# Bidirectional attention inside a two-layer encoder: the order of transposes, value matmuls and evictions within a slot

## The chip, the cores and the metric

The kernel runs on one core of one Trainium2 chip. The metric is the time of one execution on the device in microseconds. Three executions of the kernel before took 5469.95, 5459.16 and 5456.58 us, a median of 5459.16 us. Engines are named as the profile names them: PE is TensorE (PEld its weight loads), DVE VectorE, ACT ScalarE, POOL GpSimd, SP the engine that issues the DMAs.

## The reference, cut to what matters

Two layers run over a prompt of 512 tokens and a sample of 2048, each with three groups of heads: a recurrent one, an attention, and a gated one. The change touches the attention alone. It has six heads; queries and keys have 96 features, values 64, all in float32, and nothing is masked:

```python
def bidir_attention(q, k, v):
    ...
    def one_block(q_blk):
        s = jnp.einsum('bqhd,bkhd->bhqk', q_blk.astype(jnp.float32), kf) * scale
        p = jax.nn.softmax(s, axis=-1).astype(v.dtype)
        return jnp.einsum('bhqk,bkhd->bqhd', p, v)
```

Prompt and sample attend each to itself: 512 queries over 512 keys, and 2048 over 2048.

## The kernel before, in words

Each layer runs through stages with a barrier behind each: feature projection, token projection, recurrent scan, attention (`mla_attention`), output projection. In the attention stage four engines run programs of their own and meet at semaphores.

The work is cut into slots. A slot is one tile of 128 queries of one head against 2048 keys, and for each head there is one slot (s == 0) in which the four query tiles of the prompt go against 512 keys each. So there are 17 slots for a head and 102 for a layer. Four sample slots make a group (512 queries); the prompt slot is a group by itself.

PE's loop has this order in iteration n: `scores(n)`, four matmuls into the banks 0 to 3 (L1701); `turn(n - 1, x)` for x = 0 to 3, four transposes each of the exponentials of the slot before, 128 by 128 (L1708), into bank 4 for even x and bank 5 for odd x; and `weigh(g, i)` (L1724), which multiplies the values with the transposed exponentials of an older group. A call of `weigh` is two matmuls with 64 columns of weights each; the one writes partitions 0 to 63, the other 64 to 127 of bank 6, and both run side by side in the array. The list `due` gives each iteration up to two such calls, and always two where slots follow each other: none in iterations 0, 1 and 3 to 5 of a layer, two from 6 to 102. Iterations 103 and later have no turns. Behind a group's last call `turn_out` turns the sum (copied by ACT into oT) back with four transposes (L1734) in the next iteration. In the trace a score or weigh matmul of float32 is two records, a transpose one: a slot has 8 records of scores, 16 of transposes and 8 of `weigh`.

DVE takes the maxima of the scores (L1813, L1807 in a prompt slot), makes the negative bias, and evicts the odd turns (L1822). ACT evicts turn 0 (L1777), computes the exponentials in two halves of 1024 keys (L1768; in a prompt slot four of 512, L1765), evicts turn 2, and behind a group copies oT (L1795).

Who waits for whom: `scores(n)` overwrites the banks that the exponentials of slot n - 1 read, banks 0 and 1 by the first half, 2 and 3 by the second; it waits for `exps` before each of its tiles. `turn(n, x)` waits for the exponentials of its half and, since two turns share a bank, for the eviction of turn x - 2 (`act_t` for even x, `dve_t` for odd). The first call of `weigh` of a group waits for all evictions of the group's last slot and for the copy of the sum before (`o_out`); the others wait for nothing. ACT's and DVE's evictions wait for their turn (`turned`) and for the group that used the buffer before (`summed`). The exponentials wait for the maxima and for all turns of the slot two before.

Of the kernel before, what the change touches and what calls it, by code (L numbers as in the profile page):

```python
# [66 lines left out]
class Uses:  # L67
# [11 lines left out]
    def bank(self, label):  # L79
        return self.base + self.at[label] % self.banks  # L80
# [1496 lines left out]
def mla_attention(l, late, late_in, nc, d, ps, kc, col, amod, eps, ident):  # L1577
# [11 lines left out]
    def group_of(n):  # L1589
        h, s = slots[n]  # L1590
        return GROUPS * h + (1 + (s - 1) // TPG if s else 0)
# [8 lines left out]
    while at < len(pairs):  # L1600
        n, now = len(due), []
# [5 lines left out]
    def final_pair(u):  # L1607
        g, i = u
        return i == (1 if g % GROUPS == 0 else KB1 // 2 - 1)

    def summed_in(n):
        return [g for g, i in due[n] if final_pair((g, i))] if 0 <= n < len(due) else []

    def buffer_user_before(g):

        h, k = divmod(g, GROUPS)
        if k == 0:
            return g - GROUPS if h else None
        n = (GROUPS - 1) * h + k - 1 - 2
        return None if n < 0 else GROUPS * (n // (GROUPS - 1)) + n % (GROUPS - 1) + 1  # L1620

    with ExitStack() as ctx:
# [17 lines left out]
        def turned_to(g):  # L1640
            h, k = divmod(g, GROUPS)
            return PTs[((GROUPS - 1) * h + k - 1) % 2] if k else PTp

        def evict_target(n, x):
            h, s = slots[n]
            if s == 0:
                return PTp[:, 0:TPG, x * P:(x + 1) * P]
            j = (s - 1) % TPG
            return turned_to(group_of(n))[:, TPG * x:TPG * (x + 1), j * P:(j + 1) * P]
# [3 lines left out]
        with stage(nc, "in0 in1 first_in v_in0 v_in1 scored maxed exps turned act_t dve_t summed o_out o_turned normed sent0 sent1 zeroed chain") as (  # L1653
# [34 lines left out]
            @block.tensor  # L1688
            def _(pe):
                def scores(n):  # L1690
                    h, s = slots[n]
                    Q, K = Qs[h % 2], Ks[h % 2]
                    if h == 0 and s == 0:
                        pe.wait_ge(first_in, 32)
                    elif s == (1 if h == 0 else 0):
                        pe.wait_ge(arrived[h % 2], 32 * (h // 2 + 1))
                    for c in range(4):
                        if n:
                            pe.wait_ge(exps, exp_count[n - 1][c])
                        t, k0 = (c, 0) if s == 0 else (TPG - 1 + s, T0 + c * G)  # L1700
                        pe.matmul(ps[:, c, :], Q[:, t * P:(t + 1) * P], K[:, k0:k0 + G], start=True, stop=True).then_inc(scored, 1)  # L1701

                def turn(n, x):
                    pe.wait_ge(exps, exp_count[n][x])
                    if 2 * n + x // 2:
                        pe.wait_ge(dve_t if x % 2 else act_t, 2 * n + x // 2)
                    for k in range(TPG):
                        last = pe.transpose(ps[:, BANK_T + x % 2, k * P:(k + 1) * P],  # L1708
                                            pr[:, n % 2, (TPG * x + k) * P:(TPG * x + k + 1) * P], ident)
                    last.then_inc(turned, 1)  # L1710

                def weigh(g, i):
                    h, k = divmod(g, GROUPS)
                    if i == 0:
                        if k == 0:
                            pe.wait_ge(v_in[h % 2], 16 * (h // 2 + 1))
                        pe.wait_ge(act_t, 2 * (last_slot[g] + 1))
                        pe.wait_ge(dve_t, 2 * (last_slot[g] + 1))
                        if g:
                            pe.wait_ge(o_out, g)  # L1720
                    V, PT = Vs[h % 2], turned_to(g)
                    for half in range(2):
                        kb = 2 * i + half
                        last = pe.matmul(ps[DV * half:DV * half + DV, BANK_O, :], V[:, kb + (TPG if k else 0), 0:DV], PT[:, kb, :],  # L1724
                                         start=(i == 0), stop=final_pair((g, i)))
                    if final_pair((g, i)):
                        last.then_inc(summed, 1)

                def turn_out(g):
                    pe.wait_ge(o_out, g + 1)  # L1730
                    if g:
                        pe.wait_ge(normed, g)
                    for j in range(TPG):
                        last = pe.transpose(ps[:, BANK_F, j * P:(j + 1) * P], oT[:, g % 2, j * P:(j + 1) * P], ident)  # L1734
                    last.then_inc(o_turned, 1)

                for n in range(len(due) + 1):
                    now = due[n] if n < len(due) else []
                    if n < NS:
                        scores(n)  # L1740
                    turns = 1 <= n <= NS
                    if turns:
                        turn(n - 1, 0)
                    for g in summed_in(n - 1):
                        turn_out(g)
                    if turns:
                        turn(n - 1, 1)
                    for u in now:
                        weigh(*u)
                    if turns:  # L1750
                        turn(n - 1, 2)
                        turn(n - 1, 3)

            @block.scalar
            def _(a):
                def exponentials(n, half):
                    h, s = slots[n]
                    g = group_of(n) % GROUPS
                    if half == 0:
                        a.wait_ge(maxed, n + 1)  # L1760
                        if n >= 2:
                            a.wait_ge(turned, 4 * (n - 1))
                    if s == 0:
                        for j in range(2 * half, 2 * half + 2):
                            a.activation(pr[:, n % 2, j * G:(j + 1) * G], ps[:, j, :], ACT.Exp, bias=nb[:, n % 2, j:j + 1], scale=SCALE,  # L1765
                                         accum_out=sums[:, h % 2, 0, j, 0:1]).then_inc(exps, 1)
                    else:
                        a.activation(pr[:, n % 2, 2 * half * G:2 * (half + 1) * G], ps[:, 2 * half:2 * half + 2, :].rearrange("p b n -> p (b n)"),  # L1768
                                     ACT.Exp, bias=nb[:, n % 2, 0:1], scale=SCALE,
                                     accum_out=sums[:, h % 2, g, (s - 1) % TPG, half:half + 1]).then_inc(exps, 1)  # L1770

                def turned_out(n, x):
                    before = buffer_user_before(group_of(n))
                    if before is not None:
                        a.wait_ge(summed, before + 1)
                    a.wait_ge(turned, 4 * n + x + 1)
                    a.activation(evict_target(n, x), bank(BANK_T), ACT.Copy).then_inc(act_t, 1)  # L1777

                for n in range(len(due)):
                    turns = 1 <= n <= NS  # L1780
                    if n == 0:
                        a.wait_ge(zeroed, 2)
                    if turns:
                        turned_out(n - 1, 0)
                    if n < NS:
                        exponentials(n, 0)
                    if n < NS:
                        exponentials(n, 1)
                    if turns:
                        turned_out(n - 1, 2)  # L1790
                    for g in summed_in(n):
                        a.wait_ge(summed, g + 1)
                        if g >= 2:
                            a.wait_ge(o_turned, g - 1)
                        a.activation(oT[:, g % 2, :], ps[:, BANK_O, :], ACT.Copy).then_inc(o_out, 1)  # L1795
# [416 lines left out]
```

## Time and profile before

| what | value |
|---|---|
| profiled execution | 5469.95 us, its span 5467.9 us, mean granted clock 0.977 |
| median of three | 5459.16 us |
| PE busy | 5195.8 us, 95% of the span |
| DVE busy | 2824.3 us, 52% |
| ACT busy | 2067.2 us, 38% |
| attention, layer 0 | about 1627 to 2394 us |
| attention, layer 1 | about 4360 to 5128 us |
| transposes of the exponentials, L1708 | 3264 records |

Busy time is the union of an engine's records. The end of a matmul is modelled, and records overlap: a float32 matmul of 512 columns is given as 592 ns while the next one starts 429 ns behind it. How fast PE goes is therefore read from the starts. In the timeline, records of one line that follow each other are merged into one row; its length runs from the first start to the last end. The difference between the starts of two rows is what the first of them takes.

### The profile page before, as it was taken

The numbers are of one execution on the slowest core, as the hardware profiler recorded it, in microseconds if no ns is written. First come the engines' busy times: TensorE is split into PE (matmuls) and PEld (weight loads), VectorE is DVE, ScalarE is ACT, GpSimd is POOL, SyncE is SP. The second block draws the span as 40 slices with busy tenths as digits, with TensorE's granted clock in tenths as the row PEclk, the third lists the DMA queues.
The fourth block names the chain that finished last, engine by engine and source line by source line (L and its number), as shares of the span: only waits on it lengthen the run. The fifth ranks groups of instructions, "written<-read, shape, count | busy, mean of one in ns | idle before, by whom it ended". The sixth has DMA issues, their size and how long they took to land. (4 is left out here: it accounts for less than half of the span.)

```text
span 5467.9 us, 94771 instructions
## 1 busy us (share of the span) xinstructions
PE 5195.8 (95%) x38844; PEld 2846.5 (52%) x38844; DVE 2824.3 (52%) x4438; ACT 2067.2 (38%) x3470; POOL 641.8 (12%) x1110
## 2 busy tenths in 40 slices
PE   8999999989989999989989999999899799999899
PEld 3444444478865555544444444444778655555454
DVE  2221486645545555556522214776455455555565
ACT  1211555345544444421112114553455444444211
POOL 0000000044430000001100000000445300000011
PEclk9999999999999999999999998999999999999999
DMA  5311565465541111036343115654656411110353
GB/s 225 140 67 56 182 214 193 142 169 148 159 122 48 25 42 31 6 116 221 118 160 140 70 55 181 214 193 144 169 144 165 120 45 25 43 31 6 107 174 117
DMA packets 570089, 646.07 MB, mean 118 GB/s; under 512 B 228336, under 2 KB 455152, under 8 KB 559872
## 3 DMA queue, kind: packets, MB, share of 16 engines
q1 hardware_dynamic: 569072, 638.88, 37.3%
q8 instruction: 313, 5.13, 0.4%
q14 instruction: 112, 0.92, 0.1%
q10 hardware_dynamic: 592, 1.15, 0.1%
HBM read 372.77 MB, written 267.13 MB: 117 GB/s over the span
## 5 line engine op out<-in xcount | busy, mean ns | idle before, releaser
L490 PE MATMUL ps<-feat_hT,w_features 128*128 128x512 f32 x2240 | 972.5, 592 | 0.0
L808 PE MATMUL ps<-w_tokens,prep_hT 128*128 128x512 f32 (+1 forms) x1920 | 826.9, 590 | 23.3 <-DMA prep_hT<-s_ht 23.3
L1701 PE MATMUL ps<-att_K,att_Q 96*128 96x512 f32 x1632 | 744.9, 599 | 31.9 <-DMA att_K<-s_qkt 22.2
L490 PEld LDWEIGHTS ps<-feat_hT,w_features 128*128 128x128 f32 x2240 | 420.4, 190 | 505.9 <-issue 502.8
L1813 DVE TENSOR_REDUCE att_mx<-ps 128x1 f32<-128x1024 f32 x384 | 470.3, 1225 | 291.0 <-PE ps L1701 291.0
L808 PEld LDWEIGHTS ps<-w_tokens,prep_hT 128*128 128x128 f32 x1920 | 365.8, 192 | 476.1 <-issue 450.1
L2094 PE MATMUL ps<-w_out,fin_yT 128*128 128x512 f32 x1280 | 569.5, 598 | 2.5 <-DVE fin_yT L2044 2.5
L1708 PEld LDWEIGHTS ps<-kc,att_pr 128*128 128x128 f32 x3264 | 367.4, 141 | 277.4 <-issue 231.5
L1777 ACT ACTIVATE att_PT<-ps 128x512 f32<-128x512 f32 x384 | 228.9, 596 | 642.1 <-PE ps L1708 641.3
L1701 PEld LDWEIGHTS ps<-att_K,att_Q 96*128 96x128 f32 x1632 | 297.3, 192 | 334.7 <-issue 276.2
L1768 ACT ACTIVATE att_pr<-ps,att_nb 128x1024 f32<-128x1024 f32 x384 | 424.4, 1110 | 80.2 <-DVE att_nb L1815 80.1
L1708 PE MATMUL ps<-kc,att_pr 128*128 128x128 f32 x3264 | 446.5, 276 | 6.8 <-ACT att_PT L1777 2.8
L1822 DVE COPY att_PT<-ps 128x512 f32<-128x512 f32 x384 | 263.7, 687 | 277.3 <-PE ps L1708 276.6
L2094 PEld LDWEIGHTS ps<-w_out,fin_yT 128*128 128x128 f32 x1280 | 239.0, 192 | 275.3 <-issue 272.0
L1724 PE MATMUL ps<-att_PT,att_V 128*64 128x512 f32 x1536 | 370.7, 604 | 0.0
L380 ACT ACTIVATE feat_z<-ps 128x512 f32<-128x512 f32 x110 | 65.6, 596 | 603.3 <-PE ps L490 603.3
L1972 POOL TENSOR_SCALAR fin_rv<-fin_st 128x1 f32<-128x1 f32 x40 | 17.7, 443 | 1981.4 <-DVE fin_st L1990 1981.4
L419 DVE SCALAR_TENSOR_TENSOR feat_co<-feat_z,col,feat_co 128x512 f32<-128x512 f32 (+1 forms) x88 | 66.1, 751 | 300.1 <-ACT feat_co L352 300.1
L404 DVE TENSOR_SCALAR feat_hT<-ps,amod 128x512 f32<-128x512 f32 x80 | 63.9, 809 | 284.0 <-PE ps L477 283.8
L1416 DVE TENSOR_TENSOR scan_tok<-ps,scan_u 64x384 f32<-64x384 f32 x160 | 88.8, 555 | 217.4 <-PE ps L1537 188.6
L704 ACT ACTIVATE prep_st<-ps 128x512 f32<-128x512 f32 (+1 forms) x120 | 69.3, 584 | 331.0 <-PE ps L808 331.0
L1247 POOL TENSOR_SCALAR scan_ss<-scan_ss 128x2 f32<-128x2 f32 x40 | 17.6, 441 | 1474.4 <-ACT scan_csq L1290 1474.4
(226 smaller groups left out, 6794.8 us busy)
## 6 DMA issues: line engine op xcount, KB each, us to landing
s_sc<-prep_sc SPq DMA_DIRECT2D x20, 3072.0 KB, 9.2
scan_src<-s_sc SPq DMA_DIRECT2D x160, 384.0 KB, 4.9
s_qkt<-scan_qT SPq DMA_DIRECT2D x40, 576.0 KB, 4.1
fin_z<-s_zt SPq DMA_DIRECT2D x40, 576.0 KB, 5.2
s_zf<-feat_co SPq DMA_DIRECT2D x88, 256.0 KB, 2.5
s_ht<-feat_hT SPq DMA_DIRECT2D x10, 2048.0 KB, 7.9
prep_hT<-s_ht SPq DMA_DIRECT2D x40, 512.0 KB, 5.7
s_zt<-prep_st SPq DMA_DIRECT2D x80, 256.0 KB, 3.4
```

Of the source, the lines that this page charges most:

```text
L490: last = pe.matmul(b, wf[:, k, i * P:(i + 1) * P], hT[g % 2][:, k, :], start=(k == 0), stop=(k == KD - 1))
L704: a.activation(st[:, n % NB, 0:c1 - c0], ps[:, tiles.bank(pieces[n]), 0:c1 - c0], ACT.Copy).then_inc(z_out, 1)
L808: last = pe.matmul(ps[:, tiles.bank(pieces[n]), 0:c1 - c0], hT[j % NH][:, k, :], wt[:, k, c0:c1], start=(k == 0), stop=(k == KD - 1))
L1416: last = v.tensor_tensor(out_, pair(u, BA * CH)[HALF[p], :, :].rearrange("p o (m i) -> p o m i", m=BA), u0[HALF[p], s, :, :].rearrange("p ...
L1701: pe.matmul(ps[:, c, :], Q[:, t * P:(t + 1) * P], K[:, k0:k0 + G], start=True, stop=True).then_inc(scored, 1)
L1708: last = pe.transpose(ps[:, BANK_T + x % 2, k * P:(k + 1) * P], pr[:, n % 2, (TPG * x + k) * P:(TPG * x + k + 1) * P], ident)
L1724: last = pe.matmul(ps[DV * half:DV * half + DV, BANK_O, :], V[:, kb + (TPG if k else 0), 0:DV], PT[:, kb, :], start=(i == 0), stop=final_p ...
L1768: a.activation(pr[:, n % 2, 2 * half * G:2 * (half + 1) * G], ps[:, 2 * half:2 * half + 2, :].rearrange("p b n -> p (b n)"), ACT.Exp, bias ...
L1777: a.activation(evict_target(n, x), bank(BANK_T), ACT.Copy).then_inc(act_t, 1)
L1813: ch.link(v.tensor_reduce(mx[:, n % 2, half:half + 1], ps[:, 2 * half:2 * half + 2, :].rearrange("p b n -> p (b n)"), AX.X, ALU.max))
L1822: v.tensor_copy(evict_target(n, x), bank(BANK_T + 1)).then_inc(dve_t, 1)
L2094: last = pe.matmul(b, yT[n % TPG][:, k, :], wo[:, k, G * c:G * (c + 1)], start=(k == 0), stop=(k == KD - 1))
```

## The change

PE's loop: the two calls of `weigh` stood together between turn 1 and turn 2. Now the first stands between turn 0 and turn 1, the second between turn 2 and turn 3. ACT's loop: the eviction of turn 2 stood behind both halves of the exponentials, and now stands between them. DVE's loop is as before.

```diff
--- before.py
+++ after.py
@@ -1743,12 +1743,14 @@
                         turn(n - 1, 0)
                     for g in summed_in(n - 1):
                         turn_out(g)
+                    for u in now[0:1]:
+                        weigh(*u)
                     if turns:
                         turn(n - 1, 1)
-                    for u in now:
+                        turn(n - 1, 2)
+                    for u in now[1:2]:
                         weigh(*u)
                     if turns:
-                        turn(n - 1, 2)
                         turn(n - 1, 3)
 
             @block.scalar
@@ -1784,10 +1786,10 @@
                         turned_out(n - 1, 0)
                     if n < NS:
                         exponentials(n, 0)
+                    if turns:
+                        turned_out(n - 1, 2)
                     if n < NS:
                         exponentials(n, 1)
-                    if turns:
-                        turned_out(n - 1, 2)
                     for g in summed_in(n):
                         a.wait_ge(summed, g + 1)
                         if g >= 2:
```

On PE, inside the attention of layer 0, one iteration reads like this before (att0_pr are the exponentials, att0_PT0 the transposed ones, kc the constants with the identity; a call of `weigh` is two matmuls here; the waits name semaphores):

```order
L1701 MATMUL ps<-att0_K1,att0_Q1 128x512 [waits exps_124] x4
L1708 MATMUL ps<-kc,att0_pr 128x128 [waits act_t_126,exps_124]
L1708 MATMUL ps<-kc,att0_pr 128x128 x3
L1708 MATMUL ps<-kc,att0_pr 128x128 [waits dve_t_127,exps_124]
L1708 MATMUL ps<-kc,att0_pr 128x128 x3
L1724 MATMUL ps<-att0_PT0,att0_V1 64x512 x4
L1708 MATMUL ps<-kc,att0_pr 128x128 [waits act_t_126,exps_124]
L1708 MATMUL ps<-kc,att0_pr 128x128 x3
```

and like this in the changed kernel:

```order
L1701 MATMUL ps<-att0_K1,att0_Q1 128x512 [waits exps_124] x4
L1708 MATMUL ps<-kc,att0_pr 128x128 [waits act_t_126,exps_124]
L1708 MATMUL ps<-kc,att0_pr 128x128 x3
L1724 MATMUL ps<-att0_PT0,att0_V1 64x512 x2
L1708 MATMUL ps<-kc,att0_pr 128x128 [waits dve_t_127,exps_124]
L1708 MATMUL ps<-kc,att0_pr 128x128 x3
L1708 MATMUL ps<-kc,att0_pr 128x128 [waits act_t_126,exps_124]
L1708 MATMUL ps<-kc,att0_pr 128x128 x3
L1724 MATMUL ps<-att0_PT0,att0_V1 64x512 x2
L1708 MATMUL ps<-kc,att0_pr 128x128 [waits dve_t_127,exps_124]
L1708 MATMUL ps<-kc,att0_pr 128x128 x3
```

The four matmuls at L1724 that stood in one row of PE's work now stand in two rows of two, with eight transposes between them.

On ACT, in the same stage, before (L1777 evicts turns, L1768 is a half of the exponentials):

```order
L1777 ACTIVATE att0_PT1<-ps 128x4x128 [waits turned_125] x2
L1768 ACTIVATE att0_pr,att0_sums<-ps,att0_nb 128x1024 [waits turned_125,maxed_123]
L1768 ACTIVATE att0_pr,att0_sums<-ps,att0_nb 128x1024
L1777 ACTIVATE att0_PT1<-ps 128x4x128 [waits turned_125] x2
L1768 ACTIVATE att0_pr,att0_sums<-ps,att0_nb 128x1024 [waits turned_125,maxed_123]
L1768 ACTIVATE att0_pr,att0_sums<-ps,att0_nb 128x1024
```

and in the changed kernel, where the line numbers are two higher:

```order
L1779 ACTIVATE att0_PT1<-ps 128x4x128 [waits turned_125]
L1770 ACTIVATE att0_pr,att0_sums<-ps,att0_nb 128x1024 [waits turned_125,maxed_123]
L1779 ACTIVATE att0_PT1<-ps 128x4x128 [waits turned_125]
L1770 ACTIVATE att0_pr,att0_sums<-ps,att0_nb 128x1024
L1779 ACTIVATE att0_PT1<-ps 128x4x128 [waits turned_125]
L1770 ACTIVATE att0_pr,att0_sums<-ps,att0_nb 128x1024 [waits turned_125,maxed_123]
```

Of the two evictions that stood together, the one of turn 2 moved up between the two halves.

## Rows read from the trace of the kernel before

**Rows 1.** Busy time by stretch, middle of layer 0's attention; engines, granted clock, DMA share.

```profile
core 0: us, PE busy (x) PEld busy (x) DVE busy (x) ACT busy (x) POOL busy (x), PEclk, DMA share, GB/s
1676.00:2378.00 702.00, 701.74 (x3175) 364.56 (x3173) 415.69 (x610) 343.06 (x623) 0.00 (x0) 1.00 0.09 20
```

**Rows 2.** Waits in 1676 to 2378 us: who waited for whom, total, times, longest.

```profile
engine line waited for: us in total, times, longest us
ACT att_PT L1777 <- PE ps L1708: 306.6, 91, 3.7
...
DVE att_PT L1822 <- PE ps L1708: 131.5, 91, 1.8
...
PEld ps L1708 <- ACT att_pr L1768: 21.9, 27, 0.8
```

**Rows 3.** Timeline of PE, two slots: start, length, engine, line, tiles, shapes, records.

```profile
1749.99 1.04 PE L1708 MATMUL ps<-kc,att_pr 128*128 128x128 f32 x8
1750.96 1.94 PE L1724 MATMUL ps<-att_PT,att_V 128*64 128x512 f32 x8
1752.83 1.09 PE L1708 MATMUL ps<-kc,att_pr 128*128 128x128 f32 x8
1753.76 3.60 PE L1701 MATMUL ps<-att_K,att_Q 96*128 96x512 f32 x8
1757.19 1.04 PE L1708 MATMUL ps<-kc,att_pr 128*128 128x128 f32 x8
1758.16 1.94 PE L1724 MATMUL ps<-att_PT,att_V 128*64 128x512 f32 x8
1760.03 1.23 PE L1708 MATMUL ps<-kc,att_pr 128*128 128x128 f32 x8
1761.10 0.59 PE L1701 MATMUL ps<-att_K,att_Q 96*128 96x512 f32 x1
```

**Rows 4.** Timeline, the long weigh block at the end of layer 0's attention.

```profile
2383.79 7.09 PE L1724 MATMUL ps<-att_PT,att_V 128*64 128x512 f32 x32
```

**Rows 5.** Timeline of PE, start of a slot with an output turn (L1734).

```profile
1764.54 0.60 PE L1708 MATMUL ps<-kc,att_pr 128*128 128x128 f32 x4
1764.97 0.60 PE L1734 MATMUL ps<-kc,att_oT 128*128 128x128 f32 x4
1765.41 0.60 PE L1708 MATMUL ps<-kc,att_pr 128*128 128x128 f32 x4
1765.94 1.94 PE L1724 MATMUL ps<-att_PT,att_V 128*64 128x512 f32 x8
```

**Rows 6.** Timeline of the weight loads at the two joints; idle before them in brackets.

```profile
1750.96 0.20 PEld L1724 LDWEIGHTS ps<-att_PT,att_V 128*64 128x64 f32 x4 [0.17 <-issue]
...
1752.83 0.85 PEld L1708 LDWEIGHTS ps<-kc,att_pr 128*128 128x128 f32 x8 [0.81 <-issue]
```

**Rows 7.** Weigh matmuls (line 1724): records, least, median, longest ns, first and last start.

```profile
L1724 PE MATMUL ps<-att_PT,att_V x1536: 592/592/644, 1678.1 to 5124.1; 128*64 128x512 f32 x192
...
L1724 PE MATMUL ps<-att_PTp,att_V x96: 592/592/643, 1651.3 to 5029.4; 128*64 128x512 f32 x96
```

**Rows 8.** Timeline of DVE, copy of turn 1 in the prompt slot.

```profile
1759.80 0.69 DVE L1822 COPY att_PT<-ps 128x512 f32<-128x512 f32 x1
```

**Rows 9.** Timeline, turns 2 and 3 and the output turn at the end.

```profile
2381.31 1.09 PE L1708 MATMUL ps<-kc,att_pr 128*128 128x128 f32 x8
...
2383.20 0.66 PE L1734 MATMUL ps<-kc,att_oT 128*128 128x128 f32 x4 [0.80 <-ACT att_oT L1795]
```

**Rows 10.** Timeline of ACT in the first slot of Rows 3.

```profile
1750.69 0.60 ACT L1777 ACTIVATE att_PT<-ps 128x512 f32<-128x512 f32 x1 [3.41 <-PE ps L1708]
1751.70 1.11 ACT L1768 ACTIVATE att_pr<-ps,att_nb 128x1024 f32<-128x1024 f32 x1 [0.41 <-DVE att_nb L1815]
...
1752.80 1.11 ACT L1768 ACTIVATE att_pr<-ps,att_nb 128x1024 f32<-128x1024 f32 x1
...
1753.89 0.59 ACT L1777 ACTIVATE att_PT<-ps 128x512 f32<-128x512 f32 x1
```

## The prediction

> **What bounds the kernel now.** I read the attention stage first, because the change stands in no other. The busy time by stretch [rows 1] shows TensorE (PE) busy for 701.74 of the 702 us in the middle of layer 0's attention, at a granted clock of 1.00 (the 2.4 GHz level); VectorE (DVE) is busy for 415.69 and ScalarE (ACT) for 343.06. The waits of the same stretch [rows 2] say who waits for whom: ACT stands 306.6 us for transposes (L1708) and DVE 131.5 us for them. So both evicting engines have room, and PE sets the pace. Whatever makes PE's row of instructions longer is paid in full, and whatever lets ACT or DVE deliver earlier is paid for nothing, except where PE now waits.
>
> The timeline of PE [rows 3] then shows what one slot is made of. From a slot's first transpose at 1749.99 to the next slot's at 1757.19 it takes 7.20 us: turns 0 and 1 (eight transposes) 0.97, the block of four weigh matmuls (eight records) 1.87, turns 2 and 3 0.93, scores 3.43. No idle time stands before any of them, and yet they are not equally dense. Scores: 3.43 / 8 records = 0.43 us each. The one long weigh block at the layer's end [rows 4] has 32 records in pairs: (7.09 - 0.59 of the last one's own length) / 15 steps = 0.43 us a pair. Four pairs are 1.72, but the block takes 1.87: 0.15 too much. Four transposes ahead of another full-width transpose take 0.43 to 0.44 (1764.54 to 1764.97 to 1765.41) [rows 5], so eight take 0.87; ahead of a weigh block four take 0.53 (1765.41 to 1765.94) and eight 0.97, which is 0.10 more each time; behind one, eight take 0.93, 0.06 more. A weigh block thus costs 0.10 + 0.15 + 0.06 = 0.31 us beyond its matmuls, however long it is; I take 0.30, as these are differences of rounded starts. The weight loads show why [rows 6]: in the stream a load precedes its matmul, but the first load of a weigh block starts at 1750.96, with its matmul, and the first behind it at 1752.83, again with its matmul, after 0.81 us without a load. The load is not hidden where the array goes from 128 columns to two halves of 64 and back.
>
> By the Trainium skill, TensorEngine Tiling (Array Packing), section Key Properties, a change of tiling mode (not merely of tile) drains TensorE, so each split of the block brings another two drains. Its page TensorE: Matmul & The Clock Gate, section Single matmul latency, gives a constant of 398 cycles at 2.4 GHz, 166 ns, for a matmul that cannot hide its fill and drain. An estimate by that page is 2 x 0.166 = 0.33 us a block, 65 us for the 196 splits instead of the sum's 59. The trace agrees in kind and nearly in size, with 0.31 us a block.
>
> **PE, part by part.** The change keeps every instruction and splits the block of two weigh calls into two blocks, one behind turn 0, one behind turn 2. How many blocks: 1536 + 96 = 1632 records [rows 7], less 2 x 32 in the long ones, divided by 8 = 196. Each gets one more entry and one more exit: 196 x 0.30 = 58.8 us. In a new slot I expect 0.53 (turn 0), 1.01 (two pairs 0.86 + 0.15), 1.02 (turns 1 and 2: 0.87 + 0.06 + 0.10), 1.01, 0.49 (turn 3 behind a block), 3.43 (scores): 7.49 to 7.50 us. Nothing lies beside it, since PE is never idle.
>
> **What goes.** In the slot that evicts behind a prompt tile's scores, turns 2 and 3 take 1.07 instead of 0.93 (1760.03 to 1761.10) [rows 3], because turn 3 waits for DVE's copy of turn 1. This stands 5 times a layer, 10 in all. In the new order turn 3 starts 3.57 us into the slot, at 1760.76 by these times, while DVE's copy began at 1759.80 [rows 8] and takes 0.69: over at 1760.49. So 10 x 0.14 = 1.4 us go. At the layer's end the last pair of a group is followed by turns 2 and 3, ACT's eviction of turn 2 and only then its copy of oT, for which PE waits 0.80 us (1890 ns from 2381.31 to 2383.20) [rows 9]. In the new order turn 2's eviction is done before; I work out 0.3 us for turn 0 that no longer waits for the eviction before it, and 0.6 for oT: 0.9 a layer, 1.8 in all, an estimate (bounds 0 and 2 x 1.89 = 3.8). Where nothing is weighed (the first slots of a layer) PE's order is unchanged.
>
> **ACT.** Its eviction of turn 2 now stands between the two exponentials. Today the second exponential runs 1752.80 to 1753.91 and the eviction 1753.89 to 1754.48 [rows 10]; the third score tile, which overwrites the banks that the second exponential reads, starts at 1753.76 + 4 x 0.43 = 1755.48. Moved behind the eviction, the exponential ends by 1754.5, and the tile now starts 0.30 later at 1755.78: 1.28 us to spare. Does ACT stand at the eviction? Turn 2 ends at about 1749.99 + 2.4 + 0.3 = 1752.69 in the new order, and ACT is in its first exponential until 1752.81. No. Behind the eviction are queued the second exponential and, once a group, oT; PE needs these 1.3 us and over 3 us later. I cost this edit at nothing; if its cover went, each slot would pay the overshoot. DVE's copy of turn 1 comes later by about 0.8 us (turn 1 ends at about 1752.3), and ends at about 1753.1; turn 3, which reuses its bank, starts at 1753.56. That is the tightest margin, 0.4 us, and it costs nothing either.
>
> **Sum.** 58.8 - 1.4 - 1.8 = 55.6 us. The profiled execution took 5469.95 us (span 5467.9), so it would be 5525.6; it was the slowest of the three shown, 10.8 us over their median of 5459.16, so for the median I predict 5459.16 + 55.6 = 5515 us, 1.0% slower. What a measurement of this kernel can't tell from no change is 0.3%, 16 us.
>
> **Rivals.**
> 1. The gaps are waits at semaphores, not a property of the array, and the new order removes them: faster. The place is the joint behind the block, where turn 2 asks for ACT's eviction of turn 0; the profile even names ACT behind some of these loads. Then turn 2, now behind turn 1, would find it all done, and 0.15 + 0.06 us go in each of 196 slots: 41 us, 5418. Against it: the joint ahead of the block takes 0.10 whether the block waits for three semaphores (the first pair of a group, 1765.94) or for none (1758.16), and behind it 1.87 in the prompt slots too, where ACT works at other times [rows 3, 5]; the eviction had begun at 1750.69 [rows 10] and was over 1.5 us before. It decides only if the new joints take under 0.05 us. Chance 0.04.
> 2. The cost is one per slot (say, of the first switch alone), or the second load is pulled ahead of running matmuls: then 5459 less 3, 5456, no change. For it only that no block of two pairs is in this trace. A rule of the Trainium skill would lead here: TensorE: Matmul & The Clock Gate, section The mechanism, says that TensorE pulls a weight load ahead of matmuls in flight when it goes to the background buffer or another row group. Here the rows at the joints [rows 6] show both loads standing until the array is empty. Chance 0.06.
> 3. A part only: entry and start cost return, the 0.15 of the block shrinks with two pairs in it. 196 x 0.16 - 3 = +28, 5487. Chance 0.07.
> 4. The handover ACT to PE breaks: turn 2 lands so late that ACT stands at its eviction, the second exponential ends after the third score tile wants its banks. It decides from 1.3 us of lateness on; at 1.6 us it would add 196 x 0.3 = 59 us more, 5574. Against it are the margins above. Chance 0.03.
>
> **How the numbers follow.** The forecast, with 0.24 to 0.36 us a slot (the bounds are the rounding of the joints' rows and a second exit that costs as much as entry and exit of this one), holds 0.80, and its own range is 5503 to 5530. For 8 in 10 with what a median of few runs moves, I go down towards the partial case and a little up: 5498 to 5531. Faster by over 0.3%: rival 1, 0.04. Within: rival 2, 0.06. Slower: the forecast and rivals 3 and 4, 0.90.
>
> **What would show it.** In the profile after: weigh blocks of 4 records, 1.01 us from their start to the next transpose; turn 0 of 0.53 us ahead of them; slots of 7.49 to 7.50 us instead of 7.20; PE's busy share of attention still over 0.99, since the cost hides in busy time; prompt slots without the 1.07; ACT's eviction between the exponentials, unwaited. Everything outside attention unchanged. I am wrong if a slot stays at 7.20 us, if the two-pair block takes 0.86, or if PE shows idle time at L1701 or L1708 with ACT or DVE behind it.

## The result, and the profile after

The changed kernel takes 5519.53 us (median of four runs, 5514.96 to 5524.57) against 5462.31 us for the kernel before in the same set of runs: a ratio of 1.0104 with a 95% interval of 1.0087 to 1.0121. It is slower by 1.0%, 57 us; 5515 us had been predicted, within 5498 to 5531.

Its profiled execution took 5531.59 us, with a span of 5529.7. The busy time by stretch of this execution, for the middle of layer 0's attention stage, reads:

```profile
core 0: us, PE busy (x) PEld busy (x) DVE busy (x) ACT busy (x) POOL busy (x), PEclk, DMA share, GB/s
1676.00:2378.00 702.00, 701.59 (x3050) 341.11 (x3051) 405.50 (x587) 330.62 (x599) 0.00 (x0) 1.00 0.10 20
```

The same 702 us hold 3050 PE records instead of 3175 [rows 1], at the same granted clock of 1.00 and with PE just as busy. The loss lies inside busy time: no idle time of PE's matmuls accounts for it. From its first to its last PE record the attention stage takes 792.4 and 793.8 us in the two layers, where it took 764.8 and 765.7: 27.6 and 28.1 us more, 55.8 in all. The profiled executions differ by 61.6 us; the other 6 lie ahead of and between the attention stages, in code that is the same, and the stretch ahead of the first attention varies between 1619.8 and 1631.1 us over the eight profiled kernels of this study.

The timeline of PE shows one new slot. Columns are start, length, engine, line, operation, tiles, shapes and number of records; what a row takes is the difference to the next start:

```profile
1749.50 0.60 PE L1708 MATMUL ps<-kc,att_pr 128*128 128x128 f32 x4
1750.03 1.08 PE L1724 MATMUL ps<-att_PT,att_V 128*64 128x512 f32 x4
1751.04 1.09 PE L1708 MATMUL ps<-kc,att_pr 128*128 128x128 f32 x8
1752.06 1.08 PE L1724 MATMUL ps<-att_PT,att_V 128*64 128x512 f32 x4
1753.07 0.66 PE L1708 MATMUL ps<-kc,att_pr 128*128 128x128 f32 x4
1753.57 3.60 PE L1701 MATMUL ps<-att_K,att_Q 96*128 96x512 f32 x8
1757.00 0.60 PE L1708 MATMUL ps<-kc,att_pr 128*128 128x128 f32 x4
```

Turn 0 takes 0.53 us, each weigh block of two pairs 1.01, turns 1 and 2 together 1.02, turn 3 0.50, scores 3.43: 7.50 us from 1749.50 to 1757.00, where [rows 3] had 7.20. The 392 short blocks of the run all take between 1010 and 1011 ns. The first weight loads behind the two blocks, with the idle time ahead of each in brackets:

```profile
1751.04 0.86 PEld L1708 LDWEIGHTS ps<-kc,att_pr 128*128 128x128 f32 x8 [0.81 <-issue]
...
1753.07 0.42 PEld L1708 LDWEIGHTS ps<-kc,att_pr 128*128 128x128 f32 x4 [0.81 <-ACT att_pr L1770]
```

What [rows 6] showed once a slot is there twice: the load starts together with its own matmul instead of running beside the matmuls before it, so it was not hidden. The view puts one of them down to "issue" and one to ACT; both have 0.81 us of idle time ahead of them and both blocks take the same 1.01, so the name of the releaser (what the view gives as the end of the idle time) means nothing here. ACT and DVE in this slot:

```profile
1751.21 1.11 ACT L1770 ACTIVATE att_pr<-ps,att_nb 128x1024 f32<-128x1024 f32 x1 [0.42 <-DVE att_nb L1817]
...
1752.31 0.59 ACT L1779 ACTIVATE att_PT<-ps 128x512 f32<-128x512 f32 x1
1752.79 1.11 ACT L1770 ACTIVATE att_pr<-ps,att_nb 128x1024 f32<-128x1024 f32 x1
```

```profile
1751.80 0.69 DVE L1824 COPY att_PT<-ps 128x512 f32<-128x512 f32 x1 [0.63 <-PE ps L1708]
```

The eviction of turn 2 follows the first exponential with no wait in front of it. The second exponential is over at 1753.90, and the third score tile begins at 1753.57 + 1.72 = 1755.29: 1.39 us to spare. DVE's copy of turn 1 is over at 1752.49, 0.58 us ahead of turn 3.

### The profile page after: what moved, and what is told of

Read it like the earlier page. It is cut to its first block and busy times, and to the rows that moved or that the text cites. A ratio compares the mean times of both kernels' runs of the same rounds, so it can differ in the third digit from the quotient of the medians.

```text
span 5529.7 us, 94771 instructions
## 1 busy us (share of the span) xinstructions
PE 5253.9 (95%) x38844; PEld 2827.2 (51%) x38844; DVE 2836.4 (51%) x4438; ACT 2069.1 (37%) x3470; POOL 641.7 (12%) x1110
## 5 line engine op out<-in xcount | busy, mean ns | idle before, releaser
L1708 PE MATMUL ps<-kc,att_pr 128*128 128x128 f32 x3264 | 479.2, 279 | 5.3 <-DVE att_PT L1824 2.5
L1724 PE MATMUL ps<-att_PT,att_V 128*64 128x512 f32 x1536 | 411.2, 617 | 0.3
```

## The experiments

The profiled attention stages (first to last PE record, sum of both layers) are set beside the timed ratios, since they are free of what varies elsewhere. Before: 1530.4 us. Changed: 1586.2.

**TensorE's order alone.** The changed kernel with ScalarE's loop as before:

```diff
-                    if turns:
-                        turned_out(n - 1, 2)
                     if n < NS:
                         exponentials(n, 1)
+                    if turns:
+                        turned_out(n - 1, 2)
```

Expected: 

> TensorE's order is the changed one (one weigh call behind turn 0, one behind turn 2), ScalarE's order is the one of before (both exponential halves, then the eviction of turn 2). Theory, that every entry into and exit from the 64-column halves costs TensorE 0.30 us together: slots of 7.50 us, the time of the changed kernel, 1.0% over before. Rival, that the handover of ScalarE costs or hides part of it: the time leaves that of the changed kernel by more than 0.3% one way or the other.

Measured: 5514.91 us, ratio 1.0096 (1.0081 to 1.0111); attention 1588.2 us; the blocks take 1010 to 1011 ns and the slot is that of the changed kernel. So TensorE's order alone brings the whole loss. The only place where ScalarE's order is seen in the stage is its end, in the last slot with turns of each layer:

```profile
2402.25 0.66 PE L1708 MATMUL ps<-kc,att_pr 128*128 128x128 f32 x4
2403.32 0.63 PE L1708 MATMUL ps<-kc,att_pr 128*128 128x128 f32 x4 [0.41 <-ACT att_PT L1779]
2403.87 1.08 PE L1724 MATMUL ps<-att_PT,att_V 128*64 128x512 f32 x4
```

Without scores in between, turn 0 of the last slot waits for ACT's eviction of turn 2. From turn 3 to the block it takes 1.62 us here and 1.02 in the changed kernel: 0.6 us a layer.

**ScalarE's order alone.** The kernel before with the eviction of turn 2 between the two exponential halves (the same lines, moved the other way).

Expected: 

> TensorE's order is the one of before (both weigh calls between turns 1 and 2), ScalarE evicts turn 2 between the two exponential halves. Theory: 0.0% within 0.1%, slots of 7.20 us; turn 2 ends late here, so ScalarE waits some 0.7 us for it between the exponentials, and the second half ends about 0.3 us before the third score tile wants its banks. Rival, that the delayed second exponential stops the scores: slots longer by what it overshoots, 0.1 us of it would be 20 us (0.4%).

Measured: 5462.43 us, ratio 1.0004 (0.9994 to 1.0013); attention 1531.1 us. No change, as expected. A usual slot of ACT, and PE's scores beside it:

```profile
1834.87 0.60 ACT L1777 ACTIVATE att_PT<-ps 128x512 f32<-128x512 f32 x1 [1.11 <-PE ps L1708]
...
1835.05 2.74 PE L1701 MATMUL ps<-att_K,att_Q 96*128 96x512 f32 x6
...
1835.37 1.11 ACT L1768 ACTIVATE att_pr<-ps,att_nb 128x1024 f32<-128x1024 f32 x1
```

ACT does stand 1.11 us ahead of the eviction here (0.7 was expected), and the second exponential ends at 1836.48, 0.29 us before the third score tile at 1835.05 + 1.72 = 1836.77. The handover does break where the eviction is late. In another slot it began at 1753.81, 0.28 us later within the slot than usual (no run shows why), and the weight load of the third tile shows it:

```profile
1753.81 0.60 ACT L1777 ACTIVATE att_PT<-ps 128x512 f32<-128x512 f32 x1 [0.95 <-PE ps L1708]
```

```profile
1755.55 0.30 PEld L1701 LDWEIGHTS ps<-att_K,att_Q 96*128 96x128 f32 x2 [0.79 <-ACT att_pr L1768]
```

Its scores took 3.67 us instead of 3.44. The second exponential of this slot ended at 1755.41, just ahead of the time at which the third tile was due (1753.71 + 1.72 = 1755.43), and the tile still came 0.23 us late. So the handover itself needs about 0.25 us between the end of the exponential and the tile; the 0.29 of a usual slot are just enough. That happened in 2 of the 204 slots, 0.46 us in all. Rival 4's mechanism is thus real, but the changed kernel has 1.39 us where 0.25 are needed, so over 1.1 to spare.

**Half of the splits.** The changed kernel, with the calls parted only in odd iterations:

```diff
-                    for u in now[0:1]:
+                    split = n % 2
+                    for u in now[0:1] if split else []:
                         weigh(*u)
                     if turns:
                         turn(n - 1, 1)
+                    for u in [] if split else now:
+                        weigh(*u)
+                    if turns:
                         turn(n - 1, 2)
-                    for u in now[1:2]:
+                    for u in now[1:2] if split else []:
                         weigh(*u)
```

Expected: 

> The changed kernel, but the two weigh calls are parted only in iterations with an odd number (48 of 98 in a layer), and stand together between turns 1 and 2 in the others. Theory, a price per block: slots of 7.50 and 7.20 us in turn, 96 x 0.30 = 29 us over before, 0.5%. Rival, a price of the new order as a whole (once per change of pattern, or none where slots differ): near 0 or near 1.0%.

Measured: 5492.51 us, ratio 1.0055 (1.004 to 1.007); attention 1558.6 us, 28.2 more than before. The timeline of PE:

```profile
1743.67 0.60 PE L1708 MATMUL ps<-kc,att_pr 128*128 128x128 f32 x4
...
1747.74 3.60 PE L1701 MATMUL ps<-att_K,att_Q 96*128 96x512 f32 x8
1751.18 1.04 PE L1708 MATMUL ps<-kc,att_pr 128*128 128x128 f32 x8
1752.15 1.94 PE L1724 MATMUL ps<-att_PT,att_V 128*64 128x512 f32 x8
1754.02 1.09 PE L1708 MATMUL ps<-kc,att_pr 128*128 128x128 f32 x8
```

A parted slot takes 7.51 us (1743.67 to 1751.18), the next starts like those of before. With 0, 96 and 196 splits the attention takes 0, 28.2 and 55.8 us more: the price is one per block.

**Weigh matmuls of full width, joined and split.** In the kernel before and in the changed one, the two halves of 64 columns became matmuls of 128 weight columns, which add up other columns of the values, so that what the attention computes changes and only its time is read:

```diff
-                        last = pe.matmul(ps[DV * half:DV * half + DV, BANK_O, :], V[:, kb + (TPG if k else 0), 0:DV], PT[:, kb, :],
-                                         start=(i == 0), stop=final_pair((g, i)))
+                        at = min((kb + (TPG if k else 0)) * (DV + 1), NT * (DV + 1) - P)
+                        last = pe.matmul(ps[:, BANK_O, :], V[:, :, :].rearrange("p n c -> p (n c)")[:, at:at + P], PT[:, kb, :],
+                                         start=(i == 0 and half == 0), stop=(final_pair((g, i)) and half == 1))
```

Expected, joined: 

> The kernel before with weigh matmuls of 128 weight columns instead of two halves of 64: each takes the 128 columns of the value tile from its own start on, writes all 128 partitions of the bank, and both matmuls of a call add into the same sum, so what the attention computes is changed (sums of wrong columns). The halves no longer run side by side: a call takes 4 records x 0.43 = 1.72 us instead of 0.86. No joint is left where the array changes from 128 columns to 64. Slot: 3.43 + 16 x 0.109 + 8 x 0.43 = 8.6 us, 8 weigh records of 3.44 us with nothing on top; 196 x 1.4 + 14 for the long blocks = about 290 us more than before, 5.3%.

Expected, split: 

> The changed kernel with the same weigh matmuls of 128 columns (sums of wrong columns, as in the joined one). Theory, that the price of the split lies in the change between 128 and 64 columns: the same time as the joined one within 0.15%, each weigh block of 4 records 1.72 us. Rival, that any extra block of weigh matmuls costs 0.3 us (waits at the joints, change of bank or of operand): 59 us more than the joined one, 1.0%.

Measured: joined 5758.35 us, ratio 1.0539 (1.0521 to 1.0556), attention 1818.9; split 5749.36 us, ratio 1.0523 (1.0506 to 1.054), attention 1817.8. The medians lie 0.16% apart, with the split one the faster, where 0.15% had been expected as the most; but the intervals overlap, and the attention of the split one is only 1.0 us shorter. Splitting costs nothing here, where the rival had 59 us more. The timelines of PE, first joined, then split:

```profile
1753.96 1.04 PE L1708 MATMUL ps<-kc,att_pr 128*128 128x128 f32 x8
1754.83 3.60 PE L1701 MATMUL ps<-att_K,att_Q 96*128 96x512 f32 x8
1758.27 1.04 PE L1708 MATMUL ps<-kc,att_pr 128*128 128x128 f32 x8
1759.14 3.60 PE L1725 MATMUL ps<-att_PT,att_V 128*128 128x512 f32 x8
1762.58 1.04 PE L1708 MATMUL ps<-kc,att_pr 128*128 128x128 f32 x8
```

```profile
1751.75 0.60 PE L1708 MATMUL ps<-kc,att_pr 128*128 128x128 f32 x4
1752.19 1.88 PE L1725 MATMUL ps<-att_PT,att_V 128*128 128x512 f32 x4
1753.91 1.04 PE L1708 MATMUL ps<-kc,att_pr 128*128 128x128 f32 x8
1754.78 1.88 PE L1725 MATMUL ps<-att_PT,att_V 128*128 128x512 f32 x4
1756.50 0.60 PE L1708 MATMUL ps<-kc,att_pr 128*128 128x128 f32 x4
```

Every surcharge is gone: eight transposes ahead of a weigh block take 0.87 us instead of 0.97, behind one 0.87 instead of 0.93, a block of 8 records 3.44 = 8 x 0.43, a block of 4 records 1.72 = 4 x 0.43. The split one has the same semaphore waits, banks and operands' tiles at the same joints as the changed kernel. What is missing is the change between 128 columns and two halves of 64, and with it the price. The weight load behind a block is hidden here, for it starts 0.43 us ahead of the transposes at 1753.91:

```profile
1753.48 0.14 PEld L1708 LDWEIGHTS ps<-kc,att_pr 128*128 128x128 f32 x1 [0.24 <-issue]
```

Two things go away together in this pair: the weights are no longer 64 columns wide, and the halves no longer run side by side. The trace of the kernel before has a place that tells them apart. In its recurrent scan a transpose with 64 weight columns (L1555) stands alone between two of full width. First PE's rows, then the weight loads:

```profile
1365.69 0.33 PE L1554 MATMUL ps<-kc,scan_zb 128*128 128x128 f32 x1
1365.86 0.27 PE L1555 MATMUL ps<-kc,scan_zb 128*64 128x128 f32 x1
1365.97 0.27 PE L1556 MATMUL ps<-kc,scan_zb 128*128 128x128 f32 x1
```

```profile
1365.75 0.11 PEld L1555 LDWEIGHTS ps<-kc,scan_zb 128*64 128x64 f32 x1
1365.86 0.14 PEld L1556 LDWEIGHTS ps<-kc,scan_zb 128*128 128x128 f32 x1
```

Its load starts 0.11 us ahead of it, and so does the load of the full-width transpose behind it: both are hidden. The narrow transpose takes 0.11 us like any other. The 0.17 of the one before it are those of a first transpose behind halves that ran side by side (L1551 ends at this place): 165 ns, where the first transpose behind a weigh block takes 166. So, as far as transposes can show it, narrow weights alone cost nothing. The surcharge belongs to going over to halves that run side by side, and back.

**Fewer, longer blocks.** If a joint costs 0.30 us, half as many should win some. The kernel before, with this added behind the making of `due`:

```diff
+    for n in range(len(due)):
+        if len(due[n]) == 2 and due[n][0][0] % GROUPS and due[n][0][1] % 4 == 0:
+            due[n + 1], due[n] = due[n] + due[n + 1], []
```

Expected: 

> The kernel before with half as many weigh blocks: in the sample groups two iterations share one block of four calls in the second of them, 52 blocks a layer instead of 98. If the joints were all that counted, 92 x 0.30 = 28 us would be won (-0.5%). I expect a loss: a slot without a weigh block has nothing on TensorE to cover the maxima, the first exponential and the evictions, as in the first slots of a layer (2.97 us for the four turns instead of 1.75, then scores 3.54). 6.51 + 8.92 us for two slots instead of 14.40, so 92 x 1.03 = 95 us more, 1.7%.

Measured: 5541.16 us, ratio 1.0146 (1.0129 to 1.0163); attention 1607.4 us, 77.0 more than before. A loss as expected, but of 77 instead of 95. The timeline of PE, a slot without a block, one with four calls, and one that begins with an output turn:

```profile
1747.17 1.04 PE L1711 MATMUL ps<-kc,att_pr 128*128 128x128 f32 x8
1748.61 0.63 PE L1711 MATMUL ps<-kc,att_pr 128*128 128x128 f32 x4 [0.40 <-ACT att_PT L1780]
1749.59 0.63 PE L1711 MATMUL ps<-kc,att_pr 128*128 128x128 f32 x4 [0.35 <-DVE att_PT L1825]
1750.23 3.67 PE L1704 MATMUL ps<-att_K,att_Q 96*128 96x512 f32 x8
1753.73 1.04 PE L1711 MATMUL ps<-kc,att_pr 128*128 128x128 f32 x8
1754.70 3.65 PE L1727 MATMUL ps<-att_PT,att_V 128*64 128x512 f32 x16
1758.29 1.09 PE L1711 MATMUL ps<-kc,att_pr 128*128 128x128 f32 x8
...
1762.65 0.60 PE L1711 MATMUL ps<-kc,att_pr 128*128 128x128 f32 x4
1763.09 0.60 PE L1737 MATMUL ps<-kc,att_oT 128*128 128x128 f32 x4
1763.53 1.19 PE L1711 MATMUL ps<-kc,att_pr 128*128 128x128 f32 x8
1765.07 0.63 PE L1711 MATMUL ps<-kc,att_pr 128*128 128x128 f32 x4 [0.35 <-DVE att_PTp L1825]
1765.62 3.70 PE L1704 MATMUL ps<-att_K,att_Q 96*128 96x512 f32 x8
```

The two slots take 6.56 and 8.92 us (most slots without a block take 6.50). Four calls in one block take 3.59, 0.15 less than two blocks of 1.87, as the price per block says. But in the slot without a block turns 2 and 3 wait for the evictions, and from the first transpose to the scores it takes about 3 us instead of the 1.75 that its transposes need. What I had missed: where such a slot also holds an output turn, it is no longer than without (2.97 from 1762.65 to 1765.62), for the 0.44 us of the output turn fill the wait. 44 slots more than before are of this kind: 44 x 0.44 = 19 us, against the 18 that were missing.

## Why the prediction was right

**The surcharge per block.** 0.30 us, read from differences of starts. By the full-width run it is 968 - 875 = 93 ns ahead of a block, 1868 - 1718 = 150 in it, 929 - 873 = 56 behind it: 299 ns. With the 196 splits that the count of records had given, this carries the whole result; the new slots take 302 ns more than the old ones, 59 us. That the array is empty when these loads start, as the prediction has it against rival 2, no row shows: ends of matmuls are modelled, and the rows give only that a load starts together with its own matmul.

**The stalls that go.** In the prompt slot the rows of the changed kernel are

```profile
1768.08 0.66 PE L1708 MATMUL ps<-kc,att_pr 128*128 128x128 f32 x4
1768.58 3.60 PE L1701 MATMUL ps<-att_K,att_Q 96*128 96x512 f32 x8
```

and turn 3 takes the usual 0.50: 10 x 0.14 = 1.4 us, as predicted. The layer's end I had mis-sized. From the first transpose behind the last scores to the last output turn it takes 16.97 us instead of 17.77, though it holds two more splits (0.6 us), so 1.4 us a layer went where 0.9 had been predicted, 2.8 in all and not 1.8. Part of it is that oT is now copied right behind the block, since ACT's last eviction was over by then:

```profile
2412.63 0.60 ACT L1779 ACTIVATE att_PT<-ps 128x512 f32<-128x512 f32 x1 [1.44 <-PE ps L1708]
2413.59 0.60 ACT L1797 ACTIVATE att_oT<-ps 128x512 f32<-128x512 f32 x1 [0.36 <-PE ps L1724]
```

and 0.6 us of each layer is the wait for ScalarE that comes back in the first experiment. At the stage's start the first scores and their wait for keys took 0.6 us more in this execution. So 59.2 - 1.4 - 2.8 + 0.6 = 55.6 us, against 55.8 measured in the attention stages and 55.6 predicted. That the last two meet so closely is luck: the surcharge was 0.4 us more, the stalls took 1.0 more away, and the stage's start, which no term of the prediction held, gave 0.6 back. The medians of the timed runs differ by 57.2 us.

**The range.** Its upper end was added up in another way than its lower one. With 0.24 us a split and the 3.2 us that go the sum is 5503; with 0.36 and the same 3.2 it is 5527, and the 5530 of the prediction comes out only if nothing goes. The result lies inside either way.

**The margins.** ACT had been given 1.28 us to spare and has 1.39; DVE 0.4, and has 0.58. I had put DVE's copy too late. Of ACT's 1.39 the handover itself takes about 0.25, as the second experiment shows.

**The rivals.** Rival 1 (semaphore waits) and rival 2 (nothing for a second block) fall with the new slot, and the pair of full width shows what takes their place. Rival 3 (shorter blocks, smaller price) falls with the 1010 ns: 0.86 + 0.15. Rival 4 is real as a mechanism, and was shown where only ScalarE's order changes, but it needs over 1.1 us more of lateness in the changed kernel.

No run here beats the kernel before. Splitting its blocks costs their joints, and merging them takes from turns and softmax the cover that the blocks gave.

## What to carry to other kernels

Count how often TensorE goes between full-width matmuls and column halves that run side by side (a matmul that is merely narrow does not count, as L1555 shows), and price the surcharge from the starts of neighbouring rows; it does not appear as idle time, so a busy share of 1.00 proves nothing about it. When an engine is busy throughout, a reordering that only eases the engines which wait for it can win nothing but the few places where it stands. And a block of other work between dependent steps has two values, its joints and its cover: before merging blocks, look at a slot that has none.

## What the runs showed of the hardware that was not expected

That the surcharge does not depend on a block's length the prediction had taken for granted; the runs show how exactly it holds. Blocks of two, four and eight pairs of half-width matmuls take 1.01, 1.87 and 3.59 us, each 0.15 over 0.43 a pair, and over 392 blocks the time varies by 1 ns. The starts within a block show why the length is without effect: 0.05 us of the 0.15 stand between the first pair and the second (480 ns instead of 429, in every block), the other 0.10 between the last pair and the next transpose, and nothing in the middle. Not expected at all was that narrow weights alone are free, as the lone transpose at L1555 shows. And half-width pairs are still worth their joints: the full-width form has none, and its attention is 288 us longer (1818.9 against 1530.4), since its matmuls run one after the other.
